# Down projection of a transformer block: order of the accumulating weight transfers of the fourth and the sixth product

## Chip, cores and metric

One core of one Trainium2 chip runs the whole kernel as one program. The metric is the device time of one execution in microseconds (us); lower is better.

## What is computed

A transformer block with two attention branches and a SwiGLU feed-forward network, on 512 tokens of width 1024 in float32. The change lies in the last matrix product, the down projection `w_down`:

```python
def reference(x, ..., w_gate_up, w_down, ..., g_post_ffn, rel_bias):
    ...                                   # both attention branches, output projection
    h = rmsnorm(x, g_pre_ffn[l])
    g, u = jnp.split(h @ w_gate_up[l], 2, axis=-1)
    x = x + rmsnorm((jax.nn.silu(g) * u) @ w_down[l], g_post_ffn[l])
```

`silu(g) * u` is 512 x 2816 and `w_down` 2816 x 1024.

## The kernel before

**Seven products in place of eight.** The down projection is split into 2 x 2 blocks (rows and columns of `w_down`, halves of the tokens) and computed by a Strassen-like scheme with seven block products, k = 0 to 6. Each needs one combination of blocks of weights and one of activations. The weights of the seven products are, in order, the tiles `w_a11, w_a12, w_a22, w_a22, w_a22, w_a11, w_a12`: the first three as they were loaded, the last four after further blocks were added to the same tiles. So the fourth product (k = 3) reads `w_a22` after one addition, the fifth (k = 4) after two, the sixth (k = 5) `w_a11` after one, and the seventh (k = 6) `w_a12` after one.

**Groups.** Every product runs over 11 chunks of 128 rows, in four groups g = 0 to 3 of 3, 3, 3 and 2 chunks. The part number is n = 4k + g, from 0 to 27. A part of three chunks is 2 x 3 x 3 = 18 matmuls of 128x512, one of two chunks is 12. The weights of a group are 768 KB, or 512 KB for group 3.

**Split.** Matmuls run on float32r, so every operand is split into a rounded part and a rest. For part n ScalarE (ACT) rounds the weights into `wr_hi` (line 1635) and the activations into `xd_hi` (line 1641), and VectorE (DVE) forms `wr_lo` (line 2471) and `xd_lo` (line 2476); the latter counts up `parts_lo_done`, on which TensorE (PE) waits before it runs the part (line 1129). The split buffers are a ring of three, so ACT waits for part n - 3 to have been multiplied (`group_done`), and then for the weights: `block_in[g]` for the plain ones, `block_added[g]` for those with additions (line 1634).

**Additions by transfer.** SyncE (SP) loads the three plain blocks (`block`, line 672). The additions are accumulating DMAs that GpSimd (POOL) issues, since only its queue adds. `added(nth, dst, src, split_before)` issues one for each group. Before each it waits for `parts_lo_done` of the product that still reads the old contents of that group, and for a count: for nth = 0 that the third plain block is in (`block_in[3]` at 64), otherwise that the addition before it on the same counter `block_added[g]` has landed. The counter stands at 16 when this stage begins, and every landed transfer adds 16. There is one counter for each g, whatever tile is written. The sixteen additions are issued in this order, four groups each: `w_a11` (for k = 5), `w_a22` (for k = 3), `w_a22` again (for k = 4), `w_a12` (for k = 6). POOL works strictly in the order written: an addition that waits holds up all behind it.

Of the kernel before, what the change touches and what calls it, by code (L numbers as in the profile page):

```python
# [134 lines left out]
def build(nc, first, gain_cols, first_kw, rel_cols, x, w_in, w_branch_sparse, w_branch_sb, w_out, w_gate_up, w_down,  # L135
# [9 lines left out]
    def sb(name, cols, dt=F32, rows=P):  # L145

        shape = [rows] + (list(cols) if isinstance(cols, (list, tuple)) else [cols])
        t = nc.alloc_sbuf_tensor_at(name, shape, dt, offset=base + top[0])
        top[0] += -(-int(np.prod(shape[1:])) * 4 // 32) * 32
        return t  # L150
# [164 lines left out]
    w_a11 = sb("w_a11", [PAIRED, 512])  # L315
# [22 lines left out]
    w_a22 = sb("w_a22", [PAIRED, 512])  # L338
# [47 lines left out]
    def sems(*names):  # L386
        return [sem(n) for n in names]
# [56 lines left out]
    block_in, block_added = sems(*(f"block_in{g}" for g in range(4))), sems(*(f"block_added{g}" for g in range(4)))  # L444
# [38 lines left out]
    def w_group(d, k, g):  # L483
        return wdn[:, d, k, ENDS[g]:ENDS[g + 1], :]

    def group_of(block, g):
        return block[:, ENDS[g]:ENDS[g + 1], :]
# [5 lines left out]
    def slot_of(ring, n):  # L493
        return ring[n % 3][:, 0:ENDS[n % 4 + 1] - ENDS[n % 4], :]


    def w_plain(n):
        return group_of((w_a11, w_a12, w_a22, w_a22, w_a22, w_a11, w_a12)[n // 4], n % 4)

    def x_plain(n):  # L500
        k, g = n // 4, n % 4
        if k in (2, 5):
            return slot_of(x_fly, n)
        return group_of(t2n, g) if k == 4 else act_group(*{0: (0, 0), 1: (1, 0), 3: (0, 1), 6: (1, 1)}[k], g)
# [656 lines left out]
    def _(sc):  # L1161
# [114 lines left out]
        def split_value(c):  # L1276

            hi, _, slot = value_slot(c)
            sc.wait_ge(raw_in, (T_V + c) // 2 * 32 + 32)
            if c >= LAST:  # L1280
                sc.wait_ge(tile_done, T_V + c - LAST + 1 - 2 if c < LAST + 2 else T_V + c - 1)
            run(hi[:, slot, :], raw[:, (T_V + c) % 4, :], ACT.Copy).then_inc(w_hi_done, 1)
# [32 lines left out]
        def split_fill(k):  # L1315

            hi, _, slot = fill_slot(k)
            sc.wait_ge(raw_in, (T_FILL + k) // 2 * 32 + 32)
            sc.wait_ge(tile_done, T_FILL + k - 2)
            run(hi[:, slot, :], raw[:, (T_FILL + k) % 4, :], ACT.Copy).then_inc(w_hi_done, 1)  # L1320
# [299 lines left out]
        def operands_hi(n, between=None):  # L1620

            k, g = n // 4, n % 4
            if n == 0:
                sc.wait_ge(parts_lo_done, UP_PARTS)
            elif n == 1:
                sc.wait_ge(product_done, UP_PRODUCTS - 1)
            elif n == 2:
                sc.wait_ge(product_done, UP_PRODUCTS)
            else:
                sc.wait_ge(group_done, n - 2)  # L1630
            if k < 3:
                sc.wait_ge(block_in[g], 16 * (k + 2))
            else:
                sc.wait_ge(block_added[g], {5: 32, 3: 48, 4: 64, 6: 80}[k])
            run(slot_of(wr_hi, n), w_plain(n), ACT.Copy).then_inc(parts_hi_done, 1)  # L1635
            if between:
                between()
            if n == 1:
                sc.wait_ge(product_done, UP_PRODUCTS)
            sc.wait_ge(sum_made, UP_SUMS + g + 1 + {2: 8, 4: 4, 5: 12}.get(k, 0))  # L1640
            run(slot_of(xd_hi, n), x_plain(n), ACT.Copy).then_inc(parts_hi_done, 1)
# [10 lines left out]
        last_kept(p - 1, 0)  # L1652
        chain_kept(p, 1)
        operands_hi(0)
        fifth_kept(p, 1)
        gates_kept(p, 1)
# [12 lines left out]
        for n in range(1, GROUPS):  # L1669
            if n == 10:  # L1670
                nc.scalar.preload_act_table(ACT.Sqrt)
            if n == GROUPS - 1:
                square_end(0)
            if n == 1:
                operands_hi(n, last_pair)
            elif n == 5:
                operands_hi(n, lambda: kept(0, 0, bank(0), 5))
                kept(0, 1, bank(2), 7)
            elif n == 21:
                operands_hi(n, lambda: kept(4, 0, u_down[:, 0, :], 5))  # L1680
                kept(4, 1, u_down[:, 1, :], 7)
            else:
                operands_hi(n)
            for b in range(2):
                if n == 17:
                    kept(3, b, p5_down[:, b, :], 4 + 2 * b)
                if n == 25:
                    sc.wait_ge(summed_up, UP_SUMMED + 1 + b)
                    kept(5, b, u_down[:, b, :], 5 + 2 * b)
# [3 lines left out]
        for n in range(2):  # L1693
# [4 lines left out]
            k = 4 * TB - 1 + n  # L1698
            run(silu[:, n, :], bank(2 * TB - 1 - n), ACT.Square, accum_out=sumsq[:, k:k + 1]).then_inc(squared[3], 1)
        k = 4 * TB - 1  # L1700
# [10 lines left out]
    def _(gp):  # L1711
# [196 lines left out]
            nc.gpsimd.tensor_tensor(early[:, part, :], h_hi[:, part, 0:HALF], h_lo[:, part, 0:HALF],  # L1908
                                    ALU.add).then_inc(early_made, 1)

        def added(nth, dst, src, split_before):

            for g in range(4):
                gp.wait_ge(parts_lo_done, UP_PARTS + 4 * split_before + g + 1)
                if nth:
                    gp.wait_ge(block_added[g], 16 * nth + 16)
                else:
                    gp.wait_ge(block_in[3], 64)
                gp.dma_start(group_of(dst, g), src(g), accum_op=ALU.add).then_inc(block_added[g], 16)  # L1919

        added(0, w_a11, lambda g: w_group(1, 0, g), 0)
        added(1, w_a22, lambda g: w_group(1, 0, g), 2)
        added(2, w_a22, lambda g: w_group(0, 0, g), 3)
        added(3, w_a12, lambda g: group_of(w_a22, g), 1)

# [635 lines left out]
```

## Time and profile before

| | us |
|---|---|
| median of 3 runs | 736.43 (736.42 to 737.09) |
| the profiled execution, its own time | 736.68 |
| its span, first to last instruction | 734.9 |
| PE busy in the span | 728.3 (99%) |
| DVE, ACT, POOL busy | 596.7, 466.4, 260.5 |

All times below are from the span's start. The down projection runs on PE from 624.0 to 729.5, and the granted TensorE clock in it is 1.00 of full speed. The profiled execution lasted 1.8 us longer than its span; its own time is 0.25 us above the median of the runs.

### The profile page before, as it was taken

How to read it: one execution, taken by the hardware profiler on the slowest of the kernel's cores; microseconds unless marked ns; L12 is line 12 of the kernel's file. 1: busy time of each engine (PE TensorE's matmuls, PEld its weight loads, DVE VectorE, ACT ScalarE, POOL GpSimd, SP SyncE). 2: the span in 40 equal slices, each digit the busy share in tenths (PEclk: the TensorE clock that was granted, in tenths of full speed). 3: DMA queues.
4: the chain of work that ended last, by engine and by line, in shares of the span. 5: the costliest groups of instructions: out<-in, count | busy, mean ns of one | idle time of the engine just before them, and what ended most of it. 6: DMA issues, size and time to landing. Idle time of an engine off the chain costs nothing.

```text
span 734.9 us, 11111 instructions
## 1 busy us (share of the span) xinstructions
PE 728.3 (99%) x3867; PEld 627.4 (85%) x3867; DVE 596.7 (81%) x843; ACT 466.4 (63%) x733; POOL 260.5 (35%) x204
## 2 busy tenths in 40 slices
PE   9999999999999999999999999999999999999997
PEld 8788888888888888888888999999999999887885
DVE  4989989978866767359998888888888888995787
ACT  5663177777758676654485756666766666764664
POOL 4697265876777878421103400000000000043201
PEclk9999999999999999999999999999999999999999
DMA  9662444222404223268971023333333344999914
GB/s 333 191 181 65 147 120 115 57 58 59 113 9 130 65 71 111 62 185 273 280 188 34 1 83 93 111 114 114 115 113 87 93 163 157 343 174 206 213 37 116
DMA packets 111488, 95.21 MB, mean 130 GB/s; under 512 B 3664, under 2 KB 91736, under 8 KB 111448
## 3 DMA queue, kind: packets, MB, share of 16 engines
q1 hardware_dynamic: 104920, 78.96, 34.6%
q0 software_dynamic: 6368, 15.73, 11.6%
q8 instruction: 23, 0.38, 0.2%
q14 instruction: 17, 0.14, 0.1%
q10 hardware_dynamic: 160, 0.01, 0.0%
HBM read 84.97 MB, written 4.73 MB: 122 GB/s over the span
## 4 chain that ended last, share of the span: by engine, by line
PE 94%; DVE 2%; DMA 2%; issue 1%; ACT 1%; POOL 0%; POOLq 0%; DVEq 0%; ACTq 0%
PE ps L1048 13%; PE ps L710 11%; PE ps L711 11%; PE ps L712 11%; PE ps L1129 9%; PE ps L1054 6%; PE ps L732 6%; PE ps L971 4%; PE ps L777 3%; PE ps L1036 3%; PE ps L1038 3%; PE ps L1037 3%; PE ps L928 3%; PE ps L917 2%; DMA w_a<-in_w_down 2%; PE ps L991 1%
## 5 line engine op out<-in xcount | busy, mean ns | idle before, releaser
L710 PE MATMUL ps<-h_both,w_hi 128*128 128x512 f32 (+1 forms) x288 | 110.4, 383 | 0.0
L711 PE MATMUL ps<-h_both,w_hi 128*128 128x512 f32 (+1 forms) x288 | 109.1, 379 | 0.0
L712 PE MATMUL ps<-h_both,w_lo 128*128 128x512 f32 (+1 forms) x288 | 109.0, 379 | 0.0
L1919 POOL DMA_DIRECT2D w_a<-in_w_down x12 | 15.3, 1531 | 249.6 <-DMA w_a<-in_w_down 227.1
L1833 POOL TENSOR_TENSOR w_lo<-raw,w_hi 128x1024 fp32r<-128x1024 f32 x30 | 76.0, 2537 | 31.0 <-ACT w_hi L1320 30.6
L712 PEld LDWEIGHTS ps<-h_both,w_lo 128*128 128x128 f32 x288 | 54.2, 188 | 10.3
L710 PEld LDWEIGHTS ps<-h_both,w_hi 128*128 128x128 f32 x288 | 54.2, 188 | 9.1
L711 PEld LDWEIGHTS ps<-h_both,w_hi 128*128 128x128 f32 x288 | 54.3, 189 | 9.0
L2471 DVE TENSOR_TENSOR wr_lo<-w_a,wr_hi 128x1536 fp32r<-128x1536 f32 (+1 forms) x28 | 45.4, 1622 | 18.9 <-ACT wr_hi L1635 18.8
L1129 PE MATMUL ps<-wr_hi,xd_hi 128*128 128x512 f32 x154 | 60.1, 390 | 0.2 <-DVE xd_lo L2476 0.2
L1129 PE MATMUL ps<-wr_lo,xd_hi 128*128 128x512 f32 x154 | 60.0, 389 | 0.0
L1129 PE MATMUL ps<-wr_hi,xd_lo 128*128 128x512 f32 x154 | 59.9, 389 | 0.0
L1635 ACT ACTIVATE wr_hi<-w_a 128x1536 fp32r<-128x1536 f32 (+1 forms) x28 | 38.7, 1382 | 31.3 <-PE ps L1129 18.1
L1038 PE MATMUL ps<-t_both,sum_lo 128*128 128x256 f32 x160 | 45.3, 283 | 0.0
L1037 PE MATMUL ps<-t_both,sum_hi 128*128 128x256 f32 x160 | 45.2, 283 | 0.0
L1036 PE MATMUL ps<-t_both,sum_hi 128*128 128x256 f32 x160 | 45.2, 283 | 0.0
L2377 DVE TENSOR_TENSOR sum_lo<-sums,sum_hi 128x1024 fp32r<-128x1024 f32 x36 | 43.7, 1214 | 0.0
L1048 PE MATMUL ps<-h_both,quart_hi 128*128 128x512 f32 x160 | 43.3, 392 | 0.0
L2148 DVE TENSOR_TENSOR a_both<-ps,a_both 128x1280 fp32r<-128x1280 f32 x16 | 23.8, 1487 | 22.6 <-ACT a_both L1367 22.6
L1525 ACT ACTIVATE sum_hi<-sums 128x1024 fp32r<-128x1024 f32 x36 | 37.8, 1050 | 0.0
L1367 ACT ACTIVATE a_both<-ps 128x1280 fp32r<-128x1280 f32 x16 | 20.0, 1249 | 26.8 <-PE ps L917 26.8
L2370 DVE TENSOR_TENSOR quart_lo<-raw,quart_hi 128x1536 fp32r<-128x1536 f32 x20 | 35.7, 1783 | 0.7 <-ACT quart_hi L1520 0.7
(328 smaller groups left out, 2076.7 us busy)
## 6 DMA issues: line engine op xcount, KB each, us to landing
raw<-in_w_in SPq DMA_DIRECT2D x40, 512.0 KB, 4.6
raw<-in_w_gate_up SPq DMA_DIRECT2D x24, 512.0 KB, 3.8
raw<-in_w_gate_up SPq DMA_DIRECT2D x40, 256.0 KB, 4.2
w_a<-in_w_down SPq DMA_DIRECT2D x9, 768.0 KB, 6.2
w_a<-in_w_down POOLq DMA_DIRECT2D x9, 768.0 KB, 10.6
s<-in_w_out SPq DMA_DIRECT2D x3, 768.0 KB, 7.7
w_a<-w_a POOLq DMA_DIRECT2D x3, 768.0 KB, 13.2
x_t<-in_first SPq DMA_DIRECT2D x8, 256.0 KB, 6.5
```

Of the source, the lines that this page charges most:

```text
L710: mm(acc, whi_c, a_hi_, start=first, stop=False, skip_group_check=further)
L711: mm(acc, whi_c, a_lo_, start=False, stop=False, skip_group_check=further)
L712: return mm(acc, wlo_c, a_hi_, start=False, stop=last, skip_group_check=further)
L732: ins = mm(bank(2 * t + n), a[:, t * P:(t + 1) * P], w[:, slot, n * 512:(n + 1) * 512], start=first and p == 0, stop=last and p == 2)
L1036: mm(acc, hi[:, col], both[:, 0, c, :], start=False, stop=False, skip_group_check=True)
L1037: mm(acc, hi[:, col], both[:, 1, c, :], start=False, stop=False, skip_group_check=True)
L1038: ins = mm(acc, lo[:, col], both[:, 0, c, :], start=False, stop=c == KC // 2 - 1, skip_group_check=True)
L1048: ins = mm(whole, hi[:, first_col + c * P:first_col + (c + 1) * P], both[:, :, c, :], start=first and c == 0, stop=False, skip_group_check ...
L1054: ins = mm(bank(b, HALF), lo[:, first_col + c * P:first_col + (c + 1) * P], both[:, 0, c, :], start=False, stop=c == KC // 2 - 1, skip_gro ...
L1129: ins = mm(acc, x_[:, c, col], w_[:, c, :], start=first and c == 0 and i == 0, stop=n % 4 == 3 and c == size - 1 and i == 2, skip_group_ch ...
L1833: nc.gpsimd.tensor_tensor(lo[:, slot, :], raw[:, (T_FILL + k) % 4, :], hi[:, slot, :], sub).then_inc(w_lo_done, 1)
L2471: tt(slot_of(wr_lo, n), w_plain(n), slot_of(wr_hi, n), sub)
```

## The change

The sixteen additions stay the same. `added` gets a list of groups, and two pairs change places: groups 2 and 3 of `w_a11` (needed by the sixth product) are issued after the four groups of `w_a22` for the fourth product. On the counters of groups 2 and 3 `w_a22` is then the first to add and `w_a11` the second, so their counts in ACT's wait change places too, and the wait of `w_a11` groups 2 and 3 is now one for the landing of the `w_a22` addition of the same group.

```diff
             else:
-                sc.wait_ge(block_added[g], {5: 32, 3: 48, 4: 64, 6: 80}[k])
+                sc.wait_ge(block_added[g], {5: 32 if g < 2 else 48, 3: 48 if g < 2 else 32, 4: 64, 6: 80}[k])
...
-        def added(nth, dst, src, split_before):
-
-            for g in range(4):
+        def added(nth, dst, src, split_before, groups=range(4)):
+
+            for g in groups:
                 gp.wait_ge(parts_lo_done, UP_PARTS + 4 * split_before + g + 1)
                 if nth:
                     gp.wait_ge(block_added[g], 16 * nth + 16)
...
-        added(0, w_a11, lambda g: w_group(1, 0, g), 0)
-        added(1, w_a22, lambda g: w_group(1, 0, g), 2)
+
+        added(0, w_a11, lambda g: w_group(1, 0, g), 0, range(2))
+        added(1, w_a22, lambda g: w_group(1, 0, g), 2, range(2))
+        added(0, w_a22, lambda g: w_group(1, 0, g), 2, range(2, 4))
+        added(1, w_a11, lambda g: w_group(1, 0, g), 0, range(2, 4))
         added(2, w_a22, lambda g: w_group(0, 0, g), 3)
         added(3, w_a12, lambda g: group_of(w_a22, g), 1)
```

## Rows read from the trace of the kernel before

**Rows 1.** The page, part 5: busy us, mean ns, then idle before and releaser.

```profile
L1129 PE MATMUL ps<-wr_hi,xd_hi 128*128 128x512 f32 x154 | 60.1, 390 | 0.2 <-DVE xd_lo L2476 0.2
```

**Rows 2.** Busy time by stretch: PE, PEld, DVE, ACT, POOL, clock, DMA share, GB/s.

```profile
666.00:674.00 8.00, 7.83 (x35) 6.03 (x34) 5.25 (x4) 4.03 (x5) 1.64 (x2) 1.00 1.13 207
682.00:700.00 18.00, 18.00 (x81) 14.92 (x80) 14.46 (x13) 12.32 (x14) 2.57 (x3) 1.00 1.08 212
```

**Rows 3.** PE in order of time: start us, us, idle before and releaser.

```profile
672.84 0.39 PE L1129 MATMUL ps<-wr_hi,xd_lo 128*128 128x512 f32 x1
673.40 0.50 PE L1129 MATMUL ps<-wr_hi,xd_hi 128*128 128x512 f32 x1 [0.17 <-DVE xd_lo L2476]
673.74 0.40 PE L1129 MATMUL ps<-wr_lo,xd_hi 128*128 128x512 f32 x1
...
684.45 0.39 PE L1129 MATMUL ps<-wr_hi,xd_hi 128*128 128x512 f32 x1
```

**Rows 4.** Who waited for whom from 640 to 700: total us, times, longest.

```profile
POOL w_a L1919 <- DVE xd_lo L2476: 27.7, 10, 6.1
ACT wr_hi L1635 <- DMA w_a<-in_w_down: 13.3, 8, 4.2
```

**Rows 5.** ACT in order of time: weight splits of parts 12 to 17.

```profile
664.64 1.49 ACT L1635 ACTIVATE wr_hi<-w_a 128x1536 fp32r<-128x1536 f32 x1 [4.25 <-DMA w_a<-in_w_down]
...
669.20 1.49 ACT L1635 ACTIVATE wr_hi<-w_a 128x1536 fp32r<-128x1536 f32 x1 [2.34 <-DMA w_a<-in_w_down]
...
673.05 1.49 ACT L1635 ACTIVATE wr_hi<-w_a 128x1536 fp32r<-128x1536 f32 x1 [1.63 <-DMA w_a<-in_w_down]
...
675.57 1.06 ACT L1635 ACTIVATE wr_hi<-w_a 128x1024 fp32r<-128x1024 f32 x1 [0.30 <-DMA w_a<-in_w_down]
...
679.34 1.49 ACT L1635 ACTIVATE wr_hi<-w_a 128x1536 fp32r<-128x1536 f32 x1 [2.19 <-DMA w_a<-in_w_down]
...
683.15 1.49 ACT L1635 ACTIVATE wr_hi<-w_a 128x1536 fp32r<-128x1536 f32 x1 [1.59 <-DMA w_a<-in_w_down]
```

**Rows 6.** DVE in order of time: the rest of the activations of parts 13 and 16.

```profile
672.39 0.95 DVE L2476 TENSOR_TENSOR xd_lo<-act,xd_hi 128x768 fp32r<-128x768 f32 x1
...
682.54 0.95 DVE L2476 TENSOR_TENSOR xd_lo<-t2n,xd_hi 128x768 fp32r<-128x768 f32 x1
```

**Rows 7.** POOL in order of time: issues of the additions and of two output transfers.

```profile
642.67 5.21 POOL L1919 DMA_DIRECT2D w_a<-in_w_down  x4 [227.11 <-DMA w_a<-in_w_down]
651.80 1.27 POOL L1919 DMA_DIRECT2D w_a<-in_w_down  x1 [3.93 <-DVE xd_lo L2476]
655.88 1.28 POOL L1919 DMA_DIRECT2D w_a<-in_w_down  x1 [2.81 <-DVE xd_lo L2476]
659.42 1.28 POOL L1919 DMA_DIRECT2D w_a<-in_w_down  x1 [2.26 <-DVE xd_lo L2476]
661.76 1.20 POOL L1919 DMA_DIRECT2D w_a<-in_w_down  x1 [1.06 <-DVE xd_lo L2476]
...
683.63 0.86 POOL L1919 DMA_DIRECT2D w_a<-w_a  x1 [2.26 <-DVE xd_lo L2476]
...
723.27 0.86 POOL L1930 DMA_DIRECT2D out<-y_end  x1 [32.44 <-DVE y_end L2289]
725.85 0.86 POOL L1930 DMA_DIRECT2D out<-y_end  x1 [1.72 <-DVE y_end L2289]
```

**Rows 8.** Transfers: landing of the addition issued at 642.67.

```profile
DMA to landing us min/median/max: 7.6/7.6/7.6
```

**Rows 9.** Transfers: landing of the two output transfers issued at 723.27 and 725.85.

```profile
out<-y_end POOLq DMA_DIRECT2D x2, 512.0 KB, 5.6
```

**Rows 10.** Busy time by stretch, at the first addition's start and later.

```profile
644.00:645.00 1.00, 1.00 (x6) 0.84 (x5) 1.00 (x3) 0.85 (x2) 1.00 (x3) 1.00 0.55 27
651.00:661.00 10.00, 10.00 (x46) 8.28 (x45) 9.40 (x10) 7.55 (x7) 3.83 (x3) 1.00 1.13 204
```

**Rows 11.** DMA queues between 663.9 and 665.2: packets, MB, share.

```profile
q8 instruction: 1, 0.02, 4.6%
```

## The prediction, made before the changed kernel ran

> **What bounds the kernel now.** I read the page's costliest groups first, for the idle time that stands before the matmuls of the down projection, since work off TensorE counts only where it makes TensorE wait. Over 154 matmuls of its first form the whole idle time is 0.2 us [rows 1]. The busy time by stretch says the same: TensorE is busy throughout from 682 to 700, and of the eight us from 666 to 674 it lacks 0.17 [rows 2]. Then I read TensorE in order of time to find that one place and its true size. Matmuls of a part start 47 steps apart between 673.74 and 684.45, so one step is 0.228 us. Between 672.84 and 673.40 lie 0.56 us, that is 0.33 too many, and between 673.40 and 673.74 lie 0.34, or 0.11 too many [rows 3]. So **all that TensorE waits in this stage is 0.44 us**, at the start of part 13 (fourth product, group 1), where it waits for VectorE's rest `xd_lo`. The next views go back from there. The table of waits shows ScalarE held 13.3 us in eight waits by the weights' transfers, and POOL held 27.7 us in ten waits by the splits [rows 4]. ScalarE in order of time shows the starts of its splits of parts 12 to 17, each released by a landing: 664.64, 669.20, 673.05, 675.57, 679.34, 683.15 [rows 5]. I take these as the landing times of the additions of groups 0 to 3 of `w_a22` for the fourth product, and of groups 0 and 1 for the fifth. The transfers' own rows show why they land so late: between 651 and 661 the DMA engines are busy without a break (share 1.13, 204 GB/s), and still so at 682 to 700 [rows 10, 2]. The DMA engines are saturated and TensorE nearly so; the stall is the point where the first catches up with the second.
>
> **Rates needed for the sum.** In the saturated stretch 768 KB take 683.15 - 679.34 = 3.81, or 673.05 - 669.20 = 3.85; I use 3.85. The 512 KB of a group 3 take 675.57 - 673.05 = 2.52 [rows 5]. One step is longer: 669.20 - 664.64 = 4.56, 0.7 over. One instruction fetch on queue 8 falls into that stretch and takes 4.6% of the 16 engines over 1.3 us, some 0.96 us of one engine [rows 11]; a landing needs the slowest engine, so I charge these 0.7 to it and keep them, since TensorE reaches the same instructions at nearly the same time.
>
> **The change, part by part.** No transfer, no split and no matmul is added or removed; ScalarE's waits are of the same number, and their other counts cost nothing. `w_a11` groups 0 and 1 are issued as before (POOL issues four additions from 642.67 on [rows 7]; the first lands after 7.6, at 650.3 [rows 8], the second 3.85 later at 654.1).
>
> *What comes forward.* POOL's next four issues, `w_a22` groups 0 to 3, keep their times 651.80, 655.88, 659.42 and 661.76 [rows 7], because each waits for a split of the third product (nothing on PE, ACT or DVE before 661 depends on an addition). Before, 3.85 + 2.52 = 6.4 us of `w_a11` transfers stood ahead of them. Now they find a nearly empty queue, so group 1 lands by about 662 to 663.5 in place of 669.2. Part 13 may be split once part 10 is multiplied: without the stall part 13 would start at 672.84 + 0.23 = 673.07, and parts 12, 11 take 18 and 12 steps, 4.1 and 2.7, so part 10 ends at 666.3. The landing is no longer what part 13 waits for, and the stall of **0.44 us goes**: this is all that can be won, 0.06%.
>
> *What is given up.* Before, POOL had put four additions into the queue at once, so the engines never ran dry. Now each of the next additions is issued only shortly ahead of the end of the one before, and any time in which the engines stand empty is lost, since the same nine additions (`w_a11` four, `w_a22` four, `w_a22` group 0 again) must be through before part 16 can be split. Before, the ninth landed at 679.34 [rows 5]. Part 16's split then took until 682.54 + 0.95 = 683.49 [rows 6], 4.15 us, and TensorE began it at 684.45 [rows 3]; at part 13, where it waited, it began 0.06 behind the rest's end (673.40 against 672.39 + 0.95 = 673.34 [rows 3, 6]). So the slack is 684.45 - 683.49 - 0.06 = 0.90, and without the stall 0.46. With a landing later by d the end moves by **max(-0.44, d - 0.90)**.
>
> *The new wait.* `w_a11` group 2 must now wait for the landing of `w_a22` group 2, and group 3 for that of group 3. Behind them on POOL stand the additions for the fifth product. POOL starts an issue about 0.5 us after a landing: 683.15 to 683.63 [rows 5, 7]; I take 0.6. When `w_a22` group 2 lands only group 3's 512 KB (2.52) are left in the queue.
>
> *How long is a transfer from issue to landing when the queue is almost empty?* Call it C for 768 KB. The trace shows no addition started with one or two us left in the queue. From below: the first addition is issued at 642.67, and the slice 644 to 645 has a share of 0.55, half of the saturated 1.13 [rows 10], so data starts near 644.5, 1.85 after the issue, and C is at least 1.85 + 3.85 = 5.7. From above: 7.6 with engines that had stood idle [rows 8]. Nearest in kind are the two output additions of 512 KB, issued 2.58 apart, both landing 5.6 after issue [rows 7, 9]: the second was issued 3.0 before the first landed and then needed 2.58 more, no more than a saturated 512 KB (2.52). It shows C of at most 5.6 + 1.33 = 6.9 for a queue that is still running. I take 6.5, nearer to this row than to the floor, and keep 5.7 and 7.6.
>
> The sum with C = 6.5, each landing the later of "the one before + its rate" and "issue + C":
> - `w_a22` g0: 651.80 + 6.5 = 658.3 (against 654.1 + 3.85 = 657.95)
> - g1: 655.88 + 6.5 = 662.4 (662.15)
> - g2: 662.4 + 3.85 = 666.25, plus 0.7 for the fetch = 666.95
> - g3: 669.5
> - `w_a11` g2: issued 666.95 + 0.6 = 667.55, lands 674.05 (against 673.35: the engines lose 0.7)
> - `w_a11` g3: issued 670.1, lands 676.6
> - `w_a22` g0 again: its split condition (part 12) is met at about 662.2 + 4.15 = 666.4; POOL is free at 671.4; lands 680.4.
>
> So d = 680.4 - 679.34 = 1.1, and the end moves by 1.1 - 0.90 = **+0.2 us**. The stall has moved from part 13 to part 16 with some 0.6 us. Parts 17 to 19 follow: landings come every 3.85, TensorE uses a part in 4.1, so nothing is added. Their issues (splits of parts 13, 14 and 15, started at 666.3, 669.0 and 673.1, done about 4.2 later) are ahead of the queue. The sixth product's `w_a11` is needed once part 17 is multiplied (684.45 and 36 steps, 692.7) and lands by 677. The seventh product's additions land from 683.15 + 3.85 + 2.52 + 3.85 = 693.4 to 703.6 now and d later then, while its first split waits for the end of part 21 (102 steps, 707.7). Nothing else is late.
>
> **A rule of the Trainium skill at this place.** The trace has 1.85 us between issue and first data and a slow start behind it. The Trainium skill, DMA: Bandwidth & Descriptors, section "Anatomy of one DMA — SWDGE (gpsimd) path", puts a fixed cost of about 2.0 us on such a transfer and most of it behind the last byte, as the write's receipt. By that rule the lead before data would be short, the queue would not run dry, and the first rival below would hold; the cold start's 7.6 against 3.85 speaks for 3.75 of fixed cost, so the measurement decides against the page's size.
>
> **Rivals.**
> 1. *The queue never runs dry* (C of 6.2 or less). With C = 5.7 the landings are 657.95, 661.8, 666.35, 668.9, 672.7, 675.2 and 679.1, d = -0.2, the whole stall goes: -0.44 us, 736.0 on the median. For it: the second output addition ran on without a break. Against it: the engines get the first bytes 1.85 after an issue, and `w_a11` group 2 is issued only 1.95 ahead of the end.
> 2. *Every near-empty start is a cold start* (slower). With C = 7.6 the landings are 659.4, 663.5, 668.05, 670.6, then issue 668.65 gives 676.25, 678.8 and 682.6: d = 3.3, end +2.4 us, 738.8. It decides from C of about 7.1 on (there d passes 2.4, the end +1.5). Place: the wait of `w_a11` group 2, with the DMA share below 1 at 669 to 672 and TensorE idle before part 16. Against it: the output rows.
> 3. *The order does not matter*: had part 13's stall another cause than the landing, such as ScalarE or VectorE being busy, it would stay, and the end would move by 0 to +0.2: 736.4 to 736.6. VectorE is busy 5.25 of the 8 us there, against 14.46 of 18 later without any stall [rows 2], so I give it little.
>
> **How the numbers follow.** The forecast, C between 6.2 and 7.1, end -0.4 to +1.5, has 0.5; rival 1 has 0.33; rival 2 has 0.12; rival 3 has 0.05. The forecast time is 736.68 + 0.2 = 736.9 for the profiled execution and 736.6 on the median of the runs. I give 736.7. The range runs from rival 1's 736.0 to 738.1, leaving out most of rival 2. A difference of 0.2%, 1.5 us, is about what a measurement of this kernel can tell from no change. Faster by more than that has no mechanism, as TensorE waits 0.44 us in all: 0.02. Slower by more is rival 2: 0.10. Within 0.2%: 0.88.
>
> **What the profile of the changed kernel would show.** The idle time before the first matmul of part 13 gone; ScalarE's splits of parts 12 to 15 released by TensorE and no longer by landings; POOL's tenth and eleventh issues waiting for landings, at about 667.5 and 670; a dip in the DMA share near 669; and an idle of about 0.6 before part 16, near 684. If part 16 shows none, rival 1 holds; if it shows 2 us or more, rival 2. A move of over 1.5 us either way that does not lie between parts 12 and 19 would make the whole working wrong.

## The result and the profile after

The changed kernel takes 741.34 us (740.33 to 741.99, 6 runs) against 736.50 (735.98 to 737.09, 6 runs): the ratio is 1.0060, with a 95% interval of 1.0049 to 1.0071. It is 4.8 us slower. The profiled execution has a span of 740.2 against 734.9, so 5.3 us are to be found in it.

Who waited for whom from 640 to 700 (total us, times, longest), three of its lines; [rows 4] answer to the first two:

```profile
POOL w_a L1919 <- DVE xd_lo L2479: 18.5, 6, 6.5
ACT wr_hi L1635 <- DMA w_a<-in_w_down: 11.8, 4, 8.9
...
PE ps L1129 <- DVE xd_lo L2479: 3.9, 1, 3.9
```

ScalarE waits for landings four times instead of eight, but once for 8.9 us, and TensorE now waits 3.9 us for an `xd_lo`. TensorE in order of time gives the place, part 16 (the counterpart of [rows 3]):

```profile
683.75 0.39 PE L1129 MATMUL ps<-wr_hi,xd_lo 128*128 128x512 f32 x1
688.00 0.50 PE L1129 MATMUL ps<-wr_hi,xd_hi 128*128 128x512 f32 x1 [3.86 <-DVE xd_lo L2479]
688.34 0.40 PE L1129 MATMUL ps<-wr_lo,xd_hi 128*128 128x512 f32 x1
...
689.30 0.63 PE L1129 MATMUL ps<-wr_lo,xd_hi 128*128 128x512 f32 x1
689.73 0.63 PE L1129 MATMUL ps<-wr_hi,xd_lo 128*128 128x512 f32 x1
```

Between 683.75 and 688.00 lie 4.02 us more than one step of 0.23, the next step has 0.11 too many, and the ten steps from 688.34 to 692.23 take 3.89 in place of 2.28, 1.61 too many, most of them 0.43 apart. No other place of the stage has an idle step; the 0.44 us before part 13 are gone. **4.02 + 0.11 + 1.61 - 0.44 = 5.3 us**, the whole difference of the spans.

ScalarE's weight splits of parts 12 to 17, as in [rows 5]:

```profile
662.42 1.49 ACT L1635 ACTIVATE wr_hi<-w_a 128x1536 fp32r<-128x1536 f32 x1 [1.92 <-PE ps L1129]
...
666.50 1.49 ACT L1635 ACTIVATE wr_hi<-w_a 128x1536 fp32r<-128x1536 f32 x1 [1.86 <-PE ps L1129]
...
669.34 1.49 ACT L1635 ACTIVATE wr_hi<-w_a 128x1536 fp32r<-128x1536 f32 x1 [0.62 <-DMA w_a<-in_w_down]
...
673.30 1.06 ACT L1635 ACTIVATE wr_hi<-w_a 128x1024 fp32r<-128x1024 f32 x1 [1.73 <-PE ps L1129]
...
683.80 1.48 ACT L1635 ACTIVATE wr_hi<-w_a 128x1536 fp32r<-128x1536 f32 x1 [8.92 <-DMA w_a<-in_w_down]
...
687.61 1.49 ACT L1635 ACTIVATE wr_hi<-w_a 128x1536 fp32r<-128x1536 f32 x1 [1.59 <-DMA w_a<-in_w_down]
```

The fourth product's splits now follow TensorE, except part 14's. (A split's start shows a landing only where a landing released it.) The ninth addition (`w_a22` group 0 for the fifth product) lands at 683.80 in place of 679.34: d = 4.46 us. POOL's issues show the new waits (as in [rows 7]; the row of three are `w_a11` group 3 and `w_a22` groups 0 and 1 again):

```profile
651.91 1.27 POOL L1919 DMA_DIRECT2D w_a<-in_w_down  x1 [6.53 <-DVE xd_lo L2479]
655.99 1.27 POOL L1919 DMA_DIRECT2D w_a<-in_w_down  x1 [2.81 <-DVE xd_lo L2479]
659.53 1.27 POOL L1919 DMA_DIRECT2D w_a<-in_w_down  x1 [2.27 <-DVE xd_lo L2479]
661.87 1.20 POOL L1919 DMA_DIRECT2D w_a<-in_w_down  x1 [1.07 <-DVE xd_lo L2479]
669.80 1.28 POOL L1919 DMA_DIRECT2D w_a<-in_w_down  x1 [6.72 <-DMA w_a<-in_w_down]
672.34 3.83 POOL L1919 DMA_DIRECT2D w_a<-in_w_down  x3 [1.26 <-DMA w_a<-in_w_down]
```

How long these took to land, for the issues at 651.91, 655.99 and 669.80 in turn:

```profile
DMA to landing us min/median/max: 7.5/7.5/7.5
...
DMA to landing us min/median/max: 8.8/8.8/8.8
...
DMA to landing us min/median/max: 7.6/7.6/7.6
```

And the stage by stretches (PE, PEld, DVE, ACT, POOL busy, granted clock, DMA share, GB/s), the counterpart of [rows 10]:

```profile
653.00:654.00 1.00, 1.00 (x6) 0.84 (x5) 0.94 (x1) 0.98 (x3) 0.18 (x1) 1.00 0.68 115
654.00:656.00 2.00, 2.00 (x10) 1.65 (x10) 2.00 (x3) 1.99 (x2) 0.01 (x1) 1.00 0.98 112
659.00:660.00 1.00, 1.00 (x6) 0.81 (x6) 1.00 (x3) 0.54 (x2) 0.47 (x1) 1.00 0.78 131
669.00:670.00 1.00, 1.00 (x6) 0.82 (x5) 1.00 (x2) 0.66 (x1) 0.20 (x1) 1.00 0.70 125
670.00:671.00 1.00, 1.00 (x6) 0.84 (x5) 0.78 (x2) 1.00 (x2) 1.00 (x1) 1.00 0.21 41
671.00:672.00 1.00, 1.00 (x6) 0.81 (x6) 1.00 (x1) 0.57 (x1) 0.08 (x1) 1.00 0.27 20
672.00:673.00 1.00, 1.00 (x6) 0.84 (x5) 1.00 (x2) 0.00 (x0) 0.66 (x1) 1.00 0.42 63
689.00:692.00 3.00, 3.00 (x9) 2.32 (x8) 2.63 (x2) 2.38 (x5) 0.13 (x1) 0.50 1.13 207
```

There are three breaks in what was a saturated stream of 205 to 210 GB/s: at 653 to 656, at 659 and, the largest, from 669 to 674. The largest begins before the landing that POOL waits for can be answered: `w_a22` group 2 lands at about 669.2, POOL issues at 669.80, and from 669.3 to 672 the queue moves only 49 GB/s, 0.13 MB. So most of group 3's 0.52 MB had been moved before group 2 counted as landed. A lead counted up to the next landing, as in the prediction and in this document, is therefore more than the engines still have to do. The last row shows TensorE's granted clock at 0.50, which of its two levels is the lower, 1.2 GHz, for the three us behind its wait, with the DMA share and the rate as everywhere else.

### The profile page after: what moved, and what is told of

Same layout as the page of the kernel before. It is cut to its first block, busy times and chain, and to the rows that moved or that the text cites. A ratio compares the mean times of both kernels' runs of the same rounds, so it can differ in the third digit from the quotient of the medians.

```text
span 740.2 us, 11111 instructions
## 1 busy us (share of the span) xinstructions
PE 729.9 (99%) x3867; PEld 628.7 (85%) x3867; DVE 597.0 (81%) x843; ACT 466.4 (63%) x733; POOL 260.6 (35%) x204
## 4 chain that ended last, share of the span: by engine, by line
PE 92%; DMA 3%; DVE 3%; issue 1%; ACT 1%; POOL 0%; POOLq 0%; DVEq 0%; ACTq 0%
PE ps L1048 12%; PE ps L710 11%; PE ps L711 11%; PE ps L712 11%; PE ps L1129 8%; PE ps L1054 6%; PE ps L732 6%; PE ps L971 4%; PE ps L777 3%; DMA w_a<-in_w_down 3%; PE ps L1038 3%; PE ps L1036 3%; PE ps L1037 3%; PE ps L928 2%; PE ps L917 2%; PE ps L991 1%
## 5 line engine op out<-in xcount | busy, mean ns | idle before, releaser
L1129 PEld LDWEIGHTS ps<-wr_hi,xd_hi 128*128 128x128 f32 x154 | 29.2, 190 | 10.4 <-DVE xd_lo L2479 4.3
```

Of the source, the lines that this page charges most:

```text
L1129: ins = mm(acc, x_[:, c, col], w_[:, c, :], start=first and c == 0 and i == 0, stop=n % 4 == 3 and c == size - 1 and i == 2, skip_group_ch ...
```

## The experiments

Two explanations stood against each other: that the loss comes from the **new wait** alone (the break at 670), or from **late issues** as such, each addition issued with little left in the queue costing a start, whatever makes it late. A third question was how much the clock adds. Each run is compared with the kernel before, run beside it on the same chip. A lead is the time from an issue to the landing of the transfer ahead of it.

**1. The new order without the new wait.** `w_a11` groups 2 and 3 count on counters of their own. (ACT's counts and those of the later additions follow. To have two free counters, two single counters of the last steps share an older one of the same engine.)

```diff
-        added(1, w_a11, lambda g: w_group(1, 0, g), 0, range(2, 4))
+        for g in range(2, 4):
+            gp.dma_start(group_of(w_a11, g), w_group(1, 0, g), accum_op=ALU.add).then_inc(own_added[g - 2], 16)
...
```

> The changed order, but w_a11 groups 2 and 3 count on two counters of their own, so POOL issues them at about 663 without waiting for the landing of w_a22 groups 2 and 3. Theory 'new wait' (the loss is the break in the transfers near 670, and that comes from the wait alone): the break near 670 goes, the wait of TensorE before part 16 goes, and the time is that of the kernel before or up to 0.4 us less, 736.1 to 736.5. Theory 'late issues' (each of the additions issued with two or three us left in the queue costs, the starts at 654 and 659 as much as the one at 670): w_a22 group 0 lands at 659.4 and group 3 near 671.8 as in the changed kernel, then w_a11 groups 2 and 3 and the ninth addition follow without a break, 3.85 + 2.52 + 3.85 later, at 682.0 in place of 683.8. TensorE waits about 2 us before part 16 in place of 3.9, and the end is 1.7 to 3 us above the kernel before: 738.2 to 739.5.

Measured: 738.89 us against 736.96, ratio 1.0028 (1.0003 to 1.0054). The transfers from 669 to 674 run without a break (share 1.13, 206 GB/s), the ninth addition lands at 681.77, and TensorE waits once:

```profile
684.25 0.39 PE L1129 MATMUL ps<-wr_hi,xd_lo 128*128 128x512 f32 x1
685.98 0.50 PE L1129 MATMUL ps<-wr_hi,xd_hi 128*128 128x512 f32 x1 [1.34 <-DVE xd_lo L2485]
```

1.73 - 0.23 = 1.5 us before part 16 in place of 4.0, and the granted clock stays at 1.00. "New wait" alone falls: without it, a loss remains. The trace shows it better than the interval, which only just leaves out no change. In this profile TensorE enters the stage at 624.62 in place of 624.01, so 0.6 of the 2.4 us by which the ninth landing is late come from before the stage: the two early starts (their additions issued at 652.41 and 656.49 here) make it 1.8 us late, and with the wait, in the changed kernel, it is 4.4. Of the 2.1 us by which the span of 737.0 is longer, the stage has 1.1, the entry 0.6 and the time behind the last matmul 0.4.

**2. One late issue in the old order.** POOL waits for `w_a11` group 2 before the first `w_a22` addition.

```diff
+        gp.wait_ge(block_added[2], 32)
         added(1, w_a22, lambda g: w_group(1, 0, g), 2)
```

> The order of the kernel before, with one wait added on POOL: the first w_a22 addition is not issued before w_a11 group 2 has landed (658.0), when one transfer of 512 KB, 2.52 us, is left in the queue. This measures by itself what one start with about 1.9 us of lead costs, without any change of order. If such a start costs nothing (5.7 from issue to landing), w_a22 group 0 lands at 664.4 as before and the time stays at 736.4. If it takes the 7.5 of a cold start, it is issued at 658.6 and lands at 666.1, 1.5 late, and all behind it is as late: TensorE waits 1.4 us or so before part 12 (split done at 670.3, wanted at 669.0) and about 0.6 more behind it, so the end is 1.5 to 2 us later, 738.0 to 738.4, and up to 1.5 more if the granted TensorE clock falls after the wait.

Measured: 739.81 us against 736.96 (737.26 to 741.53 over 11 runs), ratio 1.0031 (1.0017 to 1.0044). The addition is issued at 658.48, a lead of 2.0 us, and lands 8.5 later; its split shows it (the second line is the split behind it), and so do the rates in the slices behind the queue's end:

```profile
667.08 1.49 ACT L1635 ACTIVATE wr_hi<-w_a 128x1536 fp32r<-128x1536 f32 x1 [6.55 <-DMA w_a<-in_w_down]
...
670.81 1.49 ACT L1635 ACTIVATE wr_hi<-w_a 128x1536 fp32r<-128x1536 f32 x1 [1.51 <-DMA w_a<-in_w_down]
```

```profile
660.00:661.00 1.00, 1.00 (x6) 0.84 (x5) 1.00 (x2) 0.53 (x1) 1.00 (x2) 1.00 1.03 47
661.00:662.00 1.00, 1.00 (x6) 0.83 (x5) 0.60 (x1) 0.00 (x0) 1.00 (x3) 1.00 0.48 57
672.00:675.00 3.00, 3.00 (x8) 2.30 (x7) 2.63 (x2) 1.36 (x3) 0.81 (x1) 0.50 1.13 207
```

So one late start, with nothing reordered, costs 2.4 us on its own landing (667.08 against 664.64), 1.0 more than I expected of a cold start, but only 1.6 on the next one (670.81 against 669.20) and on those behind. The 0.8 between them fits the instruction fetch: before, it fell behind group 0's landing and made the next step long (4.56); here it begins at 664.75, ahead of that landing, and the next step is 3.73. A single late start thus costs the stream 1.6 us, about what a cold start was expected to. TensorE waits 2.2 us before part 12, and in the profiled execution (740.23, span 738.4) the clock is at 0.50 for three us behind it. The runs scatter over 4 us; whether the clock falls in each of them isn't known. The mean clock of each run is a hint that it doesn't: 0.998 to 1.000 in the five faster runs (737.26 to 738.55), 0.996 or 0.997 in five of the six slower ones (739.81 to 741.53), 0.999 in the sixth.

**3. The wait filled with work.** The changed kernel with 15 more matmuls behind part 15, which add products a second time, so that one output bank is not the reference's.

```diff
+            if n == 15 and b:
+                for i in range(15):
+                    ins = mm(acc, x_h[:, 0, col], w_h[:, 0, :], start=False, stop=False, skip_group_check=True)
             if b:
                 ins.then_inc(group_done, 1)
```

> The changed kernel with 15 more matmuls of 128x512 behind part 15 (3.4 us), which add products already in it a second time, so the sixth product's output bank is not the reference's. They fill most of the 3.9 us in which TensorE waits for part 16; part 16's own operands come no earlier. Theory 'the clock adds to the wait': in the changed kernel the granted clock is 0.5 from 688.6 to 692 and ten matmuls start 0.43 apart in place of 0.23, 1.6 us in all; with TensorE kept busy it stays at 1.0 and the end is 1.4 to 1.7 us earlier than the changed kernel, 739.6 to 739.9. Rival (the slow matmuls are slow because of the operands or the transfers beside them, not because of the idle time): they stay slow and the time stays at 741.3.

Measured: 740.20 us against 736.96, ratio 1.0038 (1.0026 to 1.0051), where the changed kernel has 1.0060 (1.0049 to 1.0071): 0.22%, 1.6 us less. The two intervals just touch; the traces are the stronger proof. From the start of part 16 to the end of the span they have 50.6 us here and 52.2 in the changed kernel. Part 16 starts at 688.09, as in the changed kernel (688.00), and the clock stays:

```profile
684.47 3.56 PE L1133 MATMUL ps<-wr_hi,xd_hi 128*128 128x512 f32 x15
688.09 0.50 PE L1129 MATMUL ps<-wr_hi,xd_hi 128*128 128x512 f32 x1
688.43 0.39 PE L1129 MATMUL ps<-wr_lo,xd_hi 128*128 128x512 f32 x1
```

```profile
688.00:692.00 4.00, 3.93 (x18) 3.25 (x18) 2.66 (x3) 3.40 (x5) 0.88 (x2) 1.00 1.13 207
```

More work, less time: the 1.6 us belong to the clock, which falls because TensorE stood idle. It isn't the operands or the transfers beside it, which are the same here (share 1.13, 207 GB/s).

**4. Only `w_a11` group 3 behind `w_a22`, on a counter of its own.** Three transfers of `w_a11` are then ahead, and each `w_a22` addition is issued with about 6 us left in the queue.

```diff
+        added(0, w_a11, lambda g: w_group(1, 0, g), 0, range(3))
+        added(1, w_a22, lambda g: w_group(1, 0, g), 2, range(3))
+        added(0, w_a22, lambda g: w_group(1, 0, g), 2, range(3, 4))
+        gp.dma_start(group_of(w_a11, 3), w_group(1, 0, 3), accum_op=ALU.add).then_inc(own_added[1], 16)
...
```

> Only w_a11 group 3 (512 KB) is moved behind the four additions of w_a22, on a counter of its own, so three transfers of w_a11 are in the queue before w_a22 group 0 is issued with 6 us of lead. Theory 'late issues': no start finds the queue near empty, w_a22 groups 0 to 3 land 2.5 us earlier than in the kernel before (662.1, 666.7, 670.5, 673.0), part 13 no longer waits, and the ninth addition lands at 679.3 as before, in time for part 16: TensorE waits nowhere in the stage, and the time is 0.44 us less than before, 736.0, which a measurement can hardly tell. If moving a transfer of w_a11 behind w_a22 costs by itself, whatever the lead, TensorE waits before part 16 and the time is over 737.

Measured: 736.19 us against 736.96, ratio 0.9989 (0.9980 to 0.9998), and a span of 733.8 against 734.9. TensorE and the transfers are busy throughout:

```profile
650.00:680.00 30.00, 30.00 (x134) 24.83 (x133) 20.00 (x19) 17.25 (x17) 12.19 (x10) 1.00 1.13 206
680.00:700.00 20.00, 20.00 (x90) 16.57 (x89) 16.69 (x15) 14.19 (x17) 2.57 (x3) 1.00 1.08 211
```

There is no step over 0.26 us in the whole stage, and the ninth addition lands at 678.54. The gain that the order can bring, 0.44 us, is there. Of the 1.1 us between the spans 0.5 lie before the stage (TensorE enters it at 623.48 in place of 624.01) and 0.6 in it. The interval just leaves out no change, so against the kernel before the gain rests mostly on the trace. Against the changed kernel this version is clearly faster.

**5. The late issue of experiment 2, four us earlier.** POOL waits for `w_a11` group 1 (`block_added[1]` at 32) in place of group 2.

> The order of the kernel before, with one wait added on POOL: the first w_a22 addition is not issued before w_a11 group 1 has landed (654.1), when w_a11 groups 2 and 3 (3.85 + 2.52 us) are still in the queue. It is issued at 654.7 in place of 651.8, with 5.8 us of lead in place of 8.7. Theory 'late issues, only near the end of the queue': with 5.8 us of lead the engines go from one transfer to the next without a break, w_a22 group 0 lands at 664.6 as before, and the time is that of the kernel before, within 0.3 us. Rival (any addition that is not issued in one run with the ones ahead of it costs a start): it lands 1 to 3 us late, as with 1.9 us of lead, where it landed 2.4 late, and the end is 1 to 3.5 us later.

Measured: 737.05 us against 737.11, ratio 0.9996 (0.9987 to 1.0005). Issued at 654.62, it lands 10.2 later, 0.3 behind before (this profile's first addition is itself issued 0.3 later, at 642.96):

```profile
664.94 1.49 ACT L1635 ACTIVATE wr_hi<-w_a 128x1536 fp32r<-128x1536 f32 x1 [4.32 <-DMA w_a<-in_w_down]
```

With a lead of 5.8 us an issue of its own costs nothing; with 2.0 it costs a start. The rival falls.

**6. Experiment 4 on the shared counter.** Only the wait for the landing of `w_a22` group 3 is added to it.

```diff
+        added(1, w_a11, lambda g: w_group(1, 0, g), 0, range(3, 4))
```

> Only w_a11 group 3 is moved behind the additions of w_a22, as in the kernel with one group on its own counter, but on the shared counter, so POOL waits for the landing of w_a22 group 3 (672.0) before it issues it. All the starts up to there have 6 us of lead. Theory 'late issues': the wait alone is enough for most of the loss. The engines stand empty when it is issued at 672.6; it lands at about 678.8 and the ninth addition 3.85 later, at 682.7 in place of 678.5. TensorE waits about 3 us before part 16, the granted clock falls after it for 1.6 us more, and the end is 4 us later than the kernel before: 740.0 to 740.8. Rival (the loss of the changed kernel comes from the early starts at 654 and 659, the new wait adds little): the time is below 738.

Measured: 741.71 us against 737.11, ratio 1.0069 (1.0055 to 1.0083). The queue is empty from 672 to 674, the ninth addition lands at 683.40, and TensorE waits before part 16:

```profile
672.00:674.00 2.00, 2.00 (x11) 1.65 (x10) 2.00 (x2) 1.31 (x2) 0.69 (x1) 1.00 0.01 2
674.00:676.00 2.00, 2.00 (x11) 1.65 (x10) 2.00 (x3) 0.76 (x2) 2.00 (x4) 1.00 0.33 27
```

```profile
683.40 1.48 ACT L1635 ACTIVATE wr_hi<-w_a 128x1536 fp32r<-128x1536 f32 x1 [8.64 <-DMA w_a<-in_w_down]
```

The loss is 4.6 us where 4 were expected. Experiments 4 and 6 differ by one wait on POOL (and in which counters are used), and by 0.8% of the time. The trace divides the break. The rate falls from 671.0 on (20 GB/s from 671.5 to 672), but `w_a22` group 3 counts as landed only at 672.7 (11.0 behind its issue at 661.74), 1.7 later. POOL issues at 673.31, no data move before 675.2, and from 676 to 678 the mean is still only 175 GB/s.

So the landing of the ninth addition sets the end, and each way to run the queue dry delays it: two early starts by 1.8 us (1), one wait by 4.1 (6). One start with nothing reordered delays what stands behind it by 1.6 (2). The changed kernel has the early starts and a wait, but the delays don't add: it is 4.4 us in all, for its first wait ends while another transfer is still in the queue. The wait is the larger part: with the early starts alone the stage lost 1.1 us (1), with a wait alone the span is 4.9 longer (739.8 against 734.9), with both it is 5.3.

## Why the prediction was wrong

**What held.** The bound (TensorE waits 0.44 us, the DMA engines are saturated), the disappearance of the stall at part 13, that POOL's tenth and eleventh issues wait for landings (forecast for 667.55 and 670.1, both 2.2 us later, at 669.80 and 672.34), the break behind them, and part 16 as the only place where the loss appears. The price formula for a landing d late, d - 0.90, also holds: for d = 4.46 it gives 3.56 of the change, and the measured waits are 4.02 + 0.11 - 0.44 = 3.69.

**The step that failed: C.** I took 6.5 us from issue to landing for an addition that finds a nearly empty queue, from the row of the two output transfers, which move data the other way, out of SBUF, and in other sizes. Every start measured with a lead of up to 3.5 us took about as long as a cold one, or longer: 7.5, 8.8 and 7.6 in the changed kernel, 7.6 and 8.2 in experiment 1, 8.5 in experiment 2, 7.5 and 7.4 in experiment 3. The cold starts of the first addition took 7.4 to 7.8 in these profiles. The row nearest in kind was the cold start of the same transfer, [rows 8], and it should have been the likeliest value. The output row itself was also misread. The first of the two was a cold start (no data moved from 718 to 723) and took 5.6; the second, issued 3.0 before the first landed, took 5.7. It saved nothing over the cold one, and the 2.58 between the landings is just the distance of the issues. So the row showed that a start with 3 us of lead costs what a cold one of its kind costs, and for an addition of 768 KB that was 7.6. With C = 7.6, the sum's d would have been 3.3, which was rival 2.

**What C = 7.6 leaves over.** The sum of rival 2 has `w_a22` group 1 land 7.6 us after its issue and group 2 8.6 after; in the changed kernel it is 8.8 and 9.7, and this makes d 1.2 us larger than rival 2's. It isn't a law of late starts. The same starts gave 8.2 and 8.5 in experiment 1, where the sum holds for group 2 to 0.1, and 7.4 and 9.3 in experiment 3. The instruction fetch on queue 8, which the sum charged with 0.7 at group 2, is a likely part of it: the two slow landings of group 1 had it ahead of them (from 663.64 and 663.40), the quick one, at 663.9, did not (from 664.45). In the changed kernel it also took 1.4 us of an engine in place of 0.96. The rest varies from one execution to the next, and its cause stays open.

**The missing term: the clock.** A wait of TensorE was priced at its length. Behind a wait of 4 us the granted clock went to half for over three us, 1.6 us more. No row of before could show its size, for there TensorE never waits long in this stage, but the sum should have had the term. It is also why rival 2, priced at 2.4, came out at 5.3: 1.2 from the landings of groups 1 and 2 above the sum, 1.6 from the clock, 0.1 from the steps around the wait.

**The chances.** Rival 2 named mechanism, place and side, and had 0.12. The reason given against it, the output rows, was one row of another kind against one of the same kind. Slower by over 0.2% had 0.10, and happened; the range ended at 738.1 because it left rival 2 out.

**The weighed rule.** The Trainium skill's page DMA: Bandwidth & Descriptors (section "Anatomy of one DMA — SWDGE (gpsimd) path") lays most of the fixed cost behind the last byte. The traces disagree for these accumulating transfers. In experiment 6 the queue is empty when one is issued at 673.31; nothing moves until 675.2, and the mean from 674 to 676 is 27 GB/s. In the kernel before, the first addition has moved its 768 KB by 649.6, counted by the slices, and lands at 650.3 [rows 8]. So the larger part of the 3.75 us stands ahead of the last byte, where it makes a gap in the stream, and some 0.7 behind it.

## What to carry to other kernels

Where a saturated queue sets the pace, what counts is how much work is in it when the next transfer is issued: here a lead of 6 us was enough and 2 to 3.5 were not; between them nothing was tried. Before transfers are put in order of need, look at the moments of their issues, and at counters shared between them, for a counter that makes one transfer wait for another's landing empties the queue when little stands behind the awaited one. Price such a gap by the cold start of the same kind of transfer, and give a wait of TensorE a second term for the clock that may fall behind it.

## What the runs showed of the hardware

- An accumulating transfer of 768 KB from HBM takes 3.81 to 3.85 us in a running stream, and 7.4 to 8.8 from issue to landing with a lead of 2 to 3.5 us, where a cold start takes 7.4 to 7.8. Nothing is saved over a cold start. Why it is so was not tried; that data begin near 2 us behind the issue and run slowly for one or two us more is seen in the slices, the cause of the slow part isn't.
- A landing is seen later than the stream ends: the rate fell 1.7 us before the landing in experiment 6 (671.0 and 672.7), so a wait for it loses that time too.
- TensorE's granted clock stayed at 1.00 behind a wait of 1.5 us (experiment 1) and was at 0.50 for some three us behind waits of 2.2 (experiment 2), 3.7 (experiment 6) and 4.0 us (the changed kernel). It cost 1.6 us in the last, and filling the wait with useless matmuls saved it. Between 1.5 and 2.2 us nothing was tried, and each wait was seen in one profile.
